# The FFN down product as seven block products, added onto the output in memory by DMA, in place of sixteen tile products added by VectorE

## The reference, cut to what matters

```python
hn = rmsnorm(h, norm_ffn_g[l])
gate, up = jnp.split(hn @ w_ffn_up[l], 2, axis=-1)
gate = dwconv(gate, conv_ffn_w[l], conv_ffn_b[l], left=FFN_CONV // 2)
h = h + (jax.nn.silu(gate) * up) @ w_ffn_down[l]
...
return h[:, N_META:]
```

## Time and profile before

| | us |
|---|---|
| three timed runs | 1365.32, 1365.39, 1353.3 |
| median | 1365.32 |
| span of the profiled execution, first to last instruction | 1355.8 |
| one steady group of the FFN | 61.36 |
| TensorE's last matmul starts | 1352.25 |

### The profile page before, as it was taken

The page is one execution under the profiler, slowest core; times in us unless marked ns, Lnnn a source line. Parts: engine busy times, 40 slices in busy tenths (PEclk is TensorE's granted clock), DMA queues, the critical chain, the costliest instruction groups (busy, mean ns, idle before and its releaser), DMA issues.

```text
span 1355.8 us, 17820 instructions
## 1 busy us (share of the span) xinstructions
PE 1304.5 (96%) x6218; PEld 1045.2 (77%) x6218; DVE 956.6 (71%) x1452; ACT 629.6 (46%) x959; POOL 138.1 (10%) x108
## 2 busy tenths in 40 slices
PE   5999998799999999999899999999999999999998
PEld 5999997466666666687678888888888888888886
DVE  5687559777777776577878656777777766667755
ACT  6486824367777776534444233333324242333320
POOL 0000033300000001232201010110101010110101
PEclk9999899699999999999999999999999999999999
DMA  6011200000000014110021211121112112121103
GB/s 212 32 51 40 71 0 1 1 1 9 9 9 10 9 40 164 57 37 9 15 83 50 61 40 63 38 70 31 62 31 70 39 60 64 39 70 31 62 31 124
DMA packets 30569, 64.27 MB, mean 47 GB/s; under 512 B 6483, under 2 KB 7187, under 8 KB 30517
## 3 DMA queue, kind: packets, MB, share of 16 engines
q1 hardware_dynamic: 30516, 63.57, 14.5%
HBM read 59.20 MB, written 4.23 MB: 47 GB/s over the span
## 4 chain that ended last, share of the span: by engine, by line
PE 84%; DVE 7%; ACT 5%; issue 2%; POOL 1%; DMA 1%; SPq 0%; DVEq 0%; POOLq 0%; ACTq 0%
PE banks L2547 31%; PE banks L100 11%; PE banks L102 11%; PE banks L101 11%; PE banks L1914 2%; PE banks L1829 2%; PE banks L1915 2%; PE banks L1934 2%; PE banks L1916 2%; PE banks L1937 2%; PE banks L1935 2%; ACT e_f L1468 1%; DVE lam_t L1611 1%; PE banks L1793 1%; PE banks L856 1%
## 5 line engine op out<-in xcount | busy, mean ns | idle before, releaser
L2547 PE MATMUL banks<-x_hi,slot_h 128*128 128x512 f32 x616 | 245.0, 398 | 4.3 <-ACT gate L2220 3.1
L2547 PE MATMUL banks<-x_hi,slot_l 128*128 128x512 f32 x616 | 243.8, 396 | 0.0
L2547 PE MATMUL banks<-x_lo,slot_h 128*128 128x512 f32 x616 | 243.7, 396 | 0.0
L2321 DVE TENSOR_TENSOR slot_l<-up_raw,slot_h 128x512 fp32r<-128x512 f32 x127 | 101.1, 796 | 149.9 <-ACT slot_h L2178 149.1
L2178 ACT ACTIVATE slot_h<-up_raw 128x512 fp32r<-128x512 f32 x127 | 79.7, 627 | 169.7 <-PE banks L2547 169.7
L2547 PEld LDWEIGHTS banks<-x_hi,slot_h 128*128 128x128 f32 x616 | 116.0, 188 | 35.5 <-issue 3.8
L100 PE MATMUL banks<-dn_h,a_h 128*128 128x512 f32 x352 | 137.8, 392 | 2.3 <-issue 2.3
L101 PE MATMUL banks<-dn_l,a_h 128*128 128x512 f32 x352 | 137.5, 391 | 0.0
L102 PE MATMUL banks<-dn_h,a_l 128*128 128x512 f32 x352 | 137.4, 390 | 0.0
L2547 PEld LDWEIGHTS banks<-x_hi,slot_l 128*128 128x128 f32 x616 | 116.0, 188 | 26.8
L2547 PEld LDWEIGHTS banks<-x_lo,slot_h 128*128 128x128 f32 x616 | 116.0, 188 | 26.5
(11 more groups left out here) (311 smaller groups left out, 2564.8 us busy)
## 6 DMA issues: line engine op xcount, KB each, us to landing
up_raw<-in_w_up SPq DMA_DIRECT2D x88, 256.0 KB, 2.7
dn_raw<-in_w_down SPq DMA_DIRECT2D x22, 512.0 KB, 4.2
win_raw<-in_w_in SPq DMA_DIRECT2D x11, 512.0 KB, 3.2
x_tm<-in_x_tm SPq DMA_DIRECT2D x8, 512.0 KB, 4.3
wo_raw<-in_w_out SPq DMA_DIRECT2D x16, 256.0 KB, 4.0
h<-in_x_tm SPq DMA_DIRECT2D x8, 512.0 KB, 5.8
out<-h SPq DMA_DIRECT2D x16, 256.0 KB, 2.0
sum_recip<-recip SPq DMA_DIRECT2D x8, 256.0 KB, 3.5
```

Of the source, the lines that this page charges most:

```text
L2321: nc.vector.tensor_tensor(s_l[slot], x, f32(s_h[slot]), ALU.subtract).then_inc(sem["up_lo"], 1)
L2547: ins = nc.tensor.matmul(o, s[slot][:, k], xs[w], start=fresh and k == 0 and n == 0, stop=k == 3 and n == 2, skip_group_check=not fresh)
```

## The change

The down product of a group becomes a Strassen product too. Its 2 x 2 blocks are: tokens in two halves of 512, the 256 inner columns in two K tiles, the output columns in two halves of 512. The seven products `D0` to `D6` have 4 token tiles x 3 matmuls each. Products run in sums through PSUM banks 4 to 7: `D0` starts afresh, `D1`, `D2`, `D3` add on top, `D4` starts afresh, `D5` starts afresh, `D6` adds on top. After each product what stands in the four banks is one addend of one quarter of the output.

- ScalarE makes the high parts of 14 operands of 128 x 512 a group (`high_a`, `high_b`; before: 4 of 128 x 512 and 2 of 128 x 1024), and after each product copies the banks, two at a time (`stage`, 128 x 1024), to one of four staging tiles.
- VectorE makes 14 low parts (`low_a`, `low_b`) and 8 sums of blocks (`down_sum`), and no longer adds tiles onto `h` nor makes the four low parts of the activations.
- GpSimd no longer makes low parts of weights. It issues 14 DMAs a group, each of two token tiles x 512 columns (512 KB), that add a staging tile onto the output in memory.
- SP writes the whole of `h` (8 x 512 KB) to the output when it is ready, ahead of the loads of unit 1 of group 0, and no stores at the end.
- TensorE's order is `U0 U1 D0 U2 U3 D1 U4 U5 D2 U6 V0 D3 V1 V2 D4 V3 V4 D5 V5 V6 D6`, with `D` of group g-1; after the last group its own `D0` to `D6` stand alone.
- Two of the staging tiles are tiles 0 to 3 of `h`, the others tiles 4 to 7. A second use of a staging tile waits for the DMAs of its first (`added`).

```diff
+    SUM_A3, SUM_B3, SUM_A2, SUM_A1, SUM_B2, SUM_A4, SUM_B1, SUM_B4 = range(1, 9)
+    STAGE_OF = (2, 3, 0, 1, 2, 0, 3)
+    FRESH = (0, 4, 5)
...
+    def a_of(k):
+        return (part(av, "11"), s2_a, part(av, "12"), part(av, "22"), part(av, "21"), part(av, "11"), s2_a)[k]
...
+    def b_of(k):
+        return (b_block(0, 0), b_block(0, 0), b_block(0, 1), b_block(0, 0), b_block(1, 0), b_block(0, 1), b_block(1, 1))[k]
...
+        sp.wait_ge(sem["hn"], NT)
+        for i in range(XT):
+            sp.dma_start(out[P * i:P * i + P], h[:, i]).then_inc(sem["stored"], 16)
         load_unit(0, 1)
...
-        with pool.Fori(0, GROUPS) as g:
-            low_down(g)
+        def add_out(g, k):
+
+            rows, c = ((0, 0), (0, 1), (4, 1), (4, 0), (0, 0), (4, 1), (0, 1))[k]
+            b = STAGE_OF[k]
+            for p in range(2):
+                r = P * (rows + 2 * p)
+                pool.wait_ge(sem["dn_act"], down_staged(g, k, p))
+                nc.gpsimd.dma_start(out[r:r + 2 * P, HALF_D * c:HALF_D * c + HALF_D].rearrange("(i p) n -> p i n", p=P),
+                                    staged[b][:, 2 * p:2 * p + 2, :], accum_op=ALU.add).then_inc(sem["added"][b], 16)
...
+        def stage(g, k, p):
+
+            b = STAGE_OF[k]
+            if p == 0:
+                uses = stage_uses(g, k)
+                if not isinstance(uses, int) or uses > 0:
+                    act.wait_ge(sem["added"][b], 32 * uses)
+            act.wait_ge(sem["dn_mm"], down_done(g, k, 2 * p + 1))
+            nc.scalar.activation(staged[b][:, 2 * p:2 * p + 2, :], bank(4 + 2 * p, 2).rearrange("p (i n) -> p i n", i=2),
+                                 ACT.Copy).then_inc(sem["dn_act"], 1)
...
+        def down_alone(g):
+
+            high_down(g, 0)
+            high_down(g, 1)
+            for k in range(7):
+                stage(g, k, 0)
+                if k < 5:
+                    high_down(g, k + 2)
+                stage(g, k, 1)
...
+        def down(g, k):
+            pe.wait_ge(sem["dn_lo"], down_splits(g, k))
+            (a_h, a_l), (w_h, w_l) = a_slots[k % 2], b_slots[k % 2]
+            for i in range(4):
+                pe.wait_ge(sem["dn_act"], down_staged(g, k - 1, i // 2))
+                ts = slice(P * i, P * i + P)
+                terms = ((a_h, w_h), (a_h, w_l), (a_l, w_h))
+                for n, (x, w) in enumerate(terms):
+                    ins = nc.tensor.matmul(bank(4 + i), x[:, ts], w, start=k in FRESH and n == 0, stop=n == 2,
+                                           skip_group_check=k not in FRESH)
                 ins.then_inc(sem["dn_mm"], 1)
```

More of the change, by code:

```diff
@@ L2249, in silu, with unit_0 @@
             nc.scalar.activation(cv[m], cv[m], ACT.Silu).then_inc(sem["silu"], 1)
[L2251 to L2263, removed]
+        def unit_0(g, d=None):
+            if d is not None:
+                high_down(d, 0)
+            high_s3(g, 0)
+            ready(act, "prod", 4 * g)
+            read(g, 0, P1, 0, "11")
+            if d is not None:
+                high_a(d, 1)
+            read(g, 0, P5, 1, "22")
+            if d is not None:
+                stage(d, 0, 0)
+                stage(d, 0, 1)
+                high_b(d, 1)
+                high_down(d, 2)
+            high_a22(g, 0)
+            read(g, 0, P6, 2, "12")
+            high_s4(g, 0)
+            if d is not None:
+                stage(d, 1, 0)
+                stage(d, 1, 1)
+                high_down(d, 3)
+            high_a11(g, 1)
+            high_s1(g, 1)
+            high_a12(g, 1)
+            if d is not None:
+                stage(d, 2, 0)
+                stage(d, 2, 1)
+            tap(g, 0)
+            read(g, 0, P4, 6, "21")
+            high_s2(g, 1)
+            tap(g, 1)
+            if d is not None:
+                high_down(d, 4)
+                silu(g, 0)
@@ L2264, in unit, with unit_1 @@
+        def unit_1(g, d=None, more=True):
+            high_s3(g, 1)
+            if d is not None:
+                silu(g, 1)
+                act.wait_ge(sem["conv2"], 2 * g + 2)
+            read(g, 1, P1, 0, "11")
+            if d is not None:
+                high_down(d, 5)
+                stage(d, 3, 0)
+                stage(d, 3, 1)
+            read(g, 1, P5, 1, "22")
+            if d is None:
                 silu(g, 0)
                 silu(g, 1)
-            high_a22(g, a)
-            read(g, a, P6, 2, "12")
@@ L2268, in unit @@
[L2268 to L2271, removed]
-            if more:
[L2273 to L2278, removed]
-            if more:
[L2280 to L2285, removed]
+            high_a22(g, 1)
@@ L2292, in first, with group @@
         def first(g):
[L2293 to L2298, removed]
+            unit_0(g)
+            unit_1(g)
+            act.wait_ge(sem["stored"], 16 * XT)
+        def group(g):
+            unit_0(g, g - 1)
+            unit_1(g, g - 1)
         def last(g):
[L2301 to L2304, removed]
+            unit_0(g, g - 1)
+            unit_1(g, g - 1, False)
+            down_alone(g)
         over_groups(act, first, group, last)
```

355 lines of the change are left out of this document (207 added, 148 removed).

## The result

The changed kernel takes 1692.09 us (median of 4 runs, 1684.88 to 1701.28) where the kernel before takes 1360.86 (4 runs, 1353.3 to 1365.39): a ratio of 1.2451, 95% interval 1.2376 to 1.2526. The forecast was 1360 us, the range 1341 to 1400. It was wrong by 332 us, far outside the range, and on the side of rival C.

The account below looks back on a forecast made before the run. It took the number of TensorE matmuls to bound the FFN; the last down product from 1302.5, its adds from 1306.2 taking 42.4 us and 2 us landing gave span 1350.6, on the median about 1360 us, range 1341 to 1400.

Parts of the forecast that it names:

- rival C: DMA engines bound every group from 3.5 us an add: about 1440 us at 4 us, 1525 at 4.55; chance 0.17.
- TensorE, ScalarE, VectorE: Steady group: TensorE 58.6 us, 2.8 less; ScalarE 43.9 and VectorE at most 47.1 us, so neither becomes the bound.
- the tightest wait: `V2` needs the bank ScalarE's read of `V0` empties: 10.2 us plus hand-overs within 11.2 us, no stall counted.
- the half microsecond before `V2`: Slack left before `V2` in each group; no stall counted, 0 to 1.5 us a group kept for the range.
- The start: SP's write of all of `h`, 11.2 us, delays loads up to 3 us: nothing counted, up to 3 us for the range.
- The DMA engines, the disputed cost: Steady group: 14 adds at 3.03 us, 42.4 us, plus 9.1 us of weight loads, 51.5 of 58.6 us: it fits.
- The rule that an add halves the rate: For adds onto memory: two source reads halve the DMA rate, giving the same 3.03 us an add.
- The end: Last down product begins at 1302.5, 26.7 us earlier; its 14 adds, 42.4 us from 1306.2, end the span at 1350.6.
- The sum: Whole kernel: span 1350.6 against 1355.8, 5.2 us less; the median stands 9.5 us over the span, so about 1360 us.

Follow-up runs that it names:

- narrow adds: Each add of the changed kernel carries 256 of its 512 columns, half the bytes in as many rows, with 1024 bytes of descriptor space: 1465.46 us.
- pairs: The changed kernel with 1536 instead of 1024 bytes of descriptor space a partition, so that GpSimd hands out two adds at a time: 1455.61 us.

## Why the prediction was wrong, step by step

- **TensorE, ScalarE, VectorE, the tightest wait.** Right. Without adds TensorE stands still for nothing in the steady groups and the last down product starts 26.6 us earlier, within 0.1 us of the forecast's 26.7; the half microsecond before `V2` was enough.
- **The start.** Right as far as it can be told: the 26.6 us by which the last down product comes earlier hold the first group with its stores too, and nothing is missing.
- **"The DMA engines, the disputed cost": the step that failed.** It asked what an add costs the engines, took 3.03 us, and multiplied by 14: "51.5 of 58.6 us, 88%. It fits." The price was a little low but of the right size: 2.9 us go with an add's bytes by the narrow adds, and the engines are booked for 3.3 to 3.7 us (35.1% of 1453.8 us with pairs, 33.6% of 1686.1 singly). At their booked rate the adds are 46 to 51 us a group where the forecast had 42.4, and with the loads the engines are just about full, as the run with small adds and more space shows at a share of 0.95. What failed is the silent assumption that one add follows another without a gap. Only one was in flight, and each paid 3.4 us that do not depend on its bytes: 6.28 us an add, 88 us a group.
- **The rule that an add halves the rate.** The Trainium skill (Collectives: The Full Stack, Part 3, "Why ReduceScatter is half of AllGather") has an add in a collective's ring halve the rate. By the engines' booked time here it is 3.68 against 1.35 us, 2.7 times, and 2.4 times for the pairs; the halving is too kind here, but that is not what cost the time.
- **Rival C** named the sign and the path: ScalarE's copies wait for adds, TensorE for ScalarE. It priced it as full engines, 1440 to 1525 us, and mentioned "GpSimd has to hand out an add every 4.2 us" only in passing. That sentence was the whole case: it handed out one every 6.28. With that number and the first add at about 719, 154 x 6.28 gives the 1686.
- **"The end"** set 14 adds behind the last copies. In the changed kernel there is no such end: nothing after the first add matters but the count of adds. TensorE's clock fell too, a mean of 0.88 of its 2.4 GHz in the steady window where it stood still a quarter of the time, 0.68 near the end where it works 36 of 95 us (so partly at its other level of 1.2 GHz), and its matmuls took 469 instead of 392 ns; the adds alone account for the span, so it cost nothing here, and in the run with small adds and more space it is back at 1.00.
- **The sum.** The 9.5 us between the span and the median, added to every span, are no constant. Where a time and a span are on record for the same execution, they lie 1.8 to 2.1 us apart; the rest is the spread of the kernel before from one execution to the next (1353.3 to 1366.75). It decided nothing.
- **What the profile of before could have told.** Nothing on the price of a batch, since GpSimd issued no DMA in it. But the code held the number, the 1024 bytes, and with it the question how much of it an add of 256 rows takes; the answer needed a run. A range that took in "one at a time at the landing time of a 512 KB transfer", 4.2 us and more, would have given 14 x 4.2 = 58.8 us a group, already at the edge, before any price for the adding.

How far two numbers carry: with 3.4 us a batch and 1.45 us for each 256 KB in it (both from the changed kernel and the narrow adds), a pair should take 9.2 us (9.50 measured), and four halves as one batch the same 9.2. Their rounds of four take 10.2 us with 1024 bytes, where the fourth goes out late, and 8.6 us with 1536. The prices were fitted to none of these, and are good to about a tenth.

## What to carry to other kernels

A queue of transfers has two prices: the time on the engines, and the round trip divided by how many can be in flight. Where a change puts a new kind of DMA on a queue, work out both, and look for the space that its descriptors need; a share of engines below 1 is no proof of room. Adds of two tiles cost 6.28 us each one at a time and 4.75 two at a time, and the difference was 64 bytes of reserve. And where one engine is full, the relief need not be all or nothing: four of seven products in memory and three on VectorE gave what seven in memory did not.

## What the runs showed of the hardware that was not expected

- An accumulating DMA of 2 x 128 rows of 2 KB left 272 packets and took 3.3 to 3.7 us of the 16 engines and, alone, 5.8 us to land; the same as a plain write 144 packets, 1.35 us and 3.4 us. GpSimd was busy 1.2 us issuing the one, 0.73 us the other.
- With 1024 bytes a partition of descriptor space GpSimd held one such add, or three of half the rows, or two plain writes of the whole size; with 1088, 1152 and 1536 bytes two such adds, and with 1536 rounds of four of half the rows. It shows in the trace only as idle time of GpSimd put down to "issue".
- Half the bytes in as many rows landed after 4.2 us instead of 5.8, and did not let a second one in.
- More space did not make the adds flow: with 1088, 1152 and 1536 bytes a new pair went out only when both of the last had landed, 8.5 us or more after its start.
